# A mixer rewritten with its side work woven in by step, and shared kv, start and first mixers reordered, in a two-block float32 transformer kernel

## The reference

```python
for l in range(DEPTH):                                   # first block
    h = h + 0.5 * rmsnorm(swiglu(rmsnorm(h, g_pre_ffn1[l]), w_ffn1_gu[l], w_ffn1_down[l]), g_post_ffn1[l])
    h = h + rmsnorm(token_mixer(rmsnorm(h, g_pre_mix[l]), ...), g_post_mix[l])
    h = h + 0.5 * rmsnorm(swiglu(rmsnorm(h, g_pre_ffn2[l]), ...), g_post_ffn2[l])

for layer in range(DEPTH):                               # second block
    x = x + 0.5 * swiglu_2(rms_norm(x, ffn1_norm[layer]), ...)
    h, mem_n = rms_norm(x, mix_norm[layer]), rms_norm(mem, mem_norm[layer])
    x = x + (mlstm_mixer(h, mem_n, ...) if layer == 0 else dilated_mixer(h, mem_n, k_sh, v_sh, ...))
    x = x + 0.5 * swiglu_2(rms_norm(x, ffn2_norm[layer]), ...)
    if layer == 0:
        kv = rms_norm(x, kv_norm) @ w_kv                 # 1024 x 1536; k_sh normed per head, v_sh

def mlstm_mixer(h, mem_n, w_in, conv_w, gate_bias, h_gain, w_out, w_mem_kv, mq_gain, mk_gain):
    p = h @ w_in
    qk = silu(causal_conv(p[..., :2 * W], conv_w))       # W = 768, 4 taps
    v, o = p[..., 2 * W:3 * W], p[..., 3 * W:4 * W]
    gates = p[..., 4 * W:4 * W + 8] + gate_bias
    q_mem = p[..., 4 * W + 8:]
    cell = mlstm_chunkwise(heads(q), heads(k), heads(v), gates[..., :4], gates[..., 4:])
    h_a = sigmoid(o) * rms_norm(cell, h_gain)            # 4 heads of 192
    h_m = memory_cross_attention(q_mem, mem_n, w_mem_kv, mq_gain, mk_gain)
    return concatenate([h_a, h_m]) @ w_out
```

## Time and profile before

| | |
|---|---|
| three runs, us | 2742.65, 2736.28, 2741.81; median 2741.81 |
| profiled execution | 2741.48 us, span 2740.2 us |
| mean granted clock of TensorE in the span | 0.944 |
| bytes moved | 385.85 MB, mean 141 GB/s |
| ACT busy, DVE busy | 1236.9 us (45%), 1714.4 us (63%) |

### The profile page before, as it was taken

The page is one execution under the profiler, slowest core; times in us unless marked ns, Lnnn a source line. Parts: engine busy times, 40 slices in busy tenths (PEclk is TensorE's granted clock), DMA queues, the critical chain, the costliest instruction groups (busy, mean ns, idle before and its releaser), DMA issues.

```text
span 2740.2 us, 45911 instructions
## 1 busy us (share of the span) xinstructions
PE 2486.9 (91%) x18761; PEld 2345.7 (86%) x18761; DVE 1714.4 (63%) x3034; ACT 1236.9 (45%) x2101; POOL 33.5 (1%) x61
## 2 busy tenths in 40 slices
PE   7998898899999989989999986869998899868999
PEld 6997788799999977779999985758998899656999
DVE  5656667675575577667658645665764675354664
ACT  4444354454454435445446433334544554433543
POOL 2000000000000000000000000000000000000000
PEclk9998999899999999989999998878999999777999
DMA  6654433465465442356647643213755465511664
GB/s 182 176 177 118 109 86 109 117 183 177 138 186 177 136 121 78 97 142 178 189 143 200 186 136 81 75 37 91 200 185 154 125 188 188 160 44 54 185 186 138
DMA packets 589569, 385.85 MB, mean 141 GB/s; under 512 B 44555, under 2 KB 563951, under 8 KB 589232
## 3 DMA queue, kind: packets, MB, share of 16 engines
q1 hardware_dynamic: 585408, 374.00, 47.3%
q10 hardware_dynamic: 2176, 5.92, 0.6%
q0 software_dynamic: 1776, 2.98, 0.4%
HBM read 378.59 MB, written 4.19 MB: 140 GB/s over the span
## 4 chain that ended last, share of the span: by engine, by line
PE 71%; DVE 16%; ACT 6%; issue 5%; DMA 1%; SPq 0%; POOL 0%; DVEq 0%; ACTq 0%; POOLq 0%
PE bank L496 70%; DVE wlo L1674 4%; ACT whi L1130 3%; DVE a_qk L2200 1%; DVE ry L1692 1%; DVE ry L1690 1%; DMA wraw<-in_w_ffn_gu 1%; DVE stat_a L2090 1%; DVE ybuf L2088 1%; DVE smh L1950 0%; POOL g L438 0%; ACT rst L1151 0%; DVE smh L2114 0%; DVE rst L1694 0%; ACT a_qk L1512 0%
## 5 line engine op out<-in xcount | busy, mean ns | idle before, releaser
L1674 DVE TENSOR_TENSOR wlo<-wraw,whi 128x1024 fp32r<-128x1024 f32 (+3 forms) x723 | 868.7, 1207 | 433.5 <-ACT whi L1130 430.4
L1130 ACT ACTIVATE whi<-wraw 128x1024 fp32r<-128x1024 f32 (+3 forms) x723 | 748.1, 1042 | 613.2 <-DMA wraw<-in_w_ffn_gu 184.9
L496 PE MATMUL bank<-xhi,whi 128*128 128x256 f32 (+2 forms) x4024 | 617.0, 294 | 75.5 <-ACT xhi L1166 26.3
L496 PEld LDWEIGHTS bank<-xhi,whi 128*128 128x128 f32 (+1 forms) x4024 | 544.0, 193 | 101.2 <-ACT xhi L1166 30.0
L496 PE MATMUL bank<-xhi,wlo 128*128 128x256 f32 (+2 forms) x4024 | 598.5, 289 | 14.8 <-DVE wlo L1674 14.8
L496 PE MATMUL bank<-xlo,whi 128*128 128x256 f32 (+2 forms) x4024 | 582.7, 286 | 0.0
L496 PEld LDWEIGHTS bank<-xhi,wlo 128*128 128x128 f32 (+1 forms) x4024 | 542.3, 192 | 18.6 <-DVE wlo L1674 18.3
L496 PEld LDWEIGHTS bank<-xlo,whi 128*128 128x128 f32 (+1 forms) x4024 | 529.9, 189 | 0.2
L496 PE MATMUL bank<-act_hi,wlo 128*128 128x256 f32 (+1 forms) x1408 | 400.5, 284 | 0.0
L496 PE MATMUL bank<-act_lo,whi 128*128 128x256 f32 (+1 forms) x1408 | 400.5, 284 | 0.0
L496 PE MATMUL bank<-act_hi,whi 128*128 128x256 f32 (+1 forms) x1408 | 398.6, 283 | 0.0
(11 more groups left out here) (373 smaller groups left out, 1852.5 us busy)
## 6 DMA issues: line engine op xcount, KB each, us to landing
wraw<-in_w_ffn_gu SPq DMA_DIRECT2D x176, 512.0 KB, 3.9
wraw<-in_w_ffn_down SPq DMA_DIRECT2D x88, 512.0 KB, 3.2
wraw<-in_ffn_w_gate SPq DMA_DIRECT2D x88, 512.0 KB, 3.9
wraw<-in_ffn_w_up SPq DMA_DIRECT2D x88, 512.0 KB, 3.9
wraw<-in_ffn_w_down SPq DMA_DIRECT2D x88, 512.0 KB, 3.2
wraw<-in_w_in SPq DMA_DIRECT2D x80, 512.0 KB, 3.9
wraw<-in_a_w_in SPq DMA_DIRECT2D x24, 384.0 KB, 3.2
wraw<-in_w_out SPq DMA_DIRECT2D x16, 512.0 KB, 3.9
```

The source lines that it names most:

```text
L496: return E.matmul(out_, lhsT, rhs, start=first, stop=last, skip_group_check=True)
L1130: A.activation(flat(whi, u), flat(wraw, u), ACT.Copy).then_inc(S("hi"), 1)
L1674: V.tensor_tensor(flat(wlo, u), flat(wraw, u), flat(whi, u).bitcast(F32), ALU.subtract).then_inc(lo_ready[u % RING], 1)
```

## The change

Stage a is written anew. Its slabs have another order (`A_HEAD`, `A_ORDER`, `A_OUT`), by head; evictions go by `take`; turns, norms, gates, convs, silus, cells and memory attention are side chains, each bound to steps, on four `xb` buffers and buffers of their own for values and norms. Silus run once per head over two pairs of slabs. The o gate is a sigmoid on ACT over four slabs at a time. The cells keep their numerator in the bank, and the normalizer goes into the mean square, without a reciprocal. The memory attention is woven with the ao slabs. The first four aoc slabs are taken together, k by k. The split of the memory rows moves into f4 (j from 14 to 17).

Shared kv takes `KV_ORDER`, with six buffers for raw keys and squares, norms on two banks, turns on another. At the start the constants come in two parts and x in two, SP holds the third slab until they are in, only the first parameter block is turned (on its own semaphore `par1`), and x is turned k by k; the other two are turned in f0. In the mixers of the first block the alpha matmuls have banks 2 and 3, and the high and low parts stand in other places of the queues. DVE's `ahead` is one slab shorter. After stage b the low parts of f7's head come after the last `fill_low`.

```diff
+A_HEAD = [("ag", 0), ("aqk", 0), ("aqk", 1), ("aqk", 8)]
+A_ORDER = ([("aqk", 9), ("av", 0), ("aqk", 2), ("av", 1), ("aqk", 3), ("aqk", 10), ("mkv", 2), ("aqk", 11), ("aqk", 4), ("av", 2), ("aqk", 5),
+            ("aqk", 12), ("av", 3), ("aqk", 13), ("aqk", 6), ("av", 4), ("aqk", 7), ("aqk", 14), ("aq", 0), ("aqk", 15), ("mkv", 0), ("av", 5),
+            ("aq", 1), ("mkv", 1), ("mkv", 3)] + [("ao", i) for i in range(8)])
+A_OUT = [("aoc", 0), ("aoc", 1), ("aoc", 2), ("aoc", 3), ("aom", 0), ("aom", 1), ("aoc", 4), ("aoc", 5), ("aom", 2), ("aoc", 6), ("aoc", 7), ("aom", 3)]
+A_TAKEN = {key: i for i, key in enumerate(A_HEAD + A_ORDER)}
+A_CONV = [i for name, i in A_HEAD + A_ORDER if name == "aqk"]
...
+A_CONV_STEP = [2, 2, 3, 3] + [A_STEP["aqk", i] + 1 for i in A_CONV[4:]]
+A_CELL_STEP = (5, 12, 18, 24)
+A_MEM_STEP = 26
+A_NORM_BANK = (7, 7, 7, 2)
+KV_ORDER = [0, 1, 2, 3, 6, 4, 7, 5, 8, 9, 10, 11]
+KV_TURN = (3, 5, 7, 8, 9, 10)
 
...
                 Y.wait_ge(S("used"), u - RING + 1)
+            elif u == 2:
+                Y.wait_ge(S("in"), 64)
             for src, c0 in pieces:
...
-                        E.wait_ge(S("evac"), c.first + 1)
+                        E.wait_ge(S("evac"), c.first + 4)
                         for q in range(2):
-                            b = next_bank()
-                            mm(bank[b][:, 0:T1], wau[:, L, q * P:q * P + P], rst2[0:GATE_RANK, :], True, True).then_inc(S("wau"), 1)
+                            mm(bank[2 + q][:, 0:T1], wau[:, L, q * P:q * P + P], rst2[0:GATE_RANK, :], True, True).then_inc(S("wau"), 1)
...
+                E.wait_ge(S("a_cn"), 4)
+                E.wait_ge(S("a_rs"), 4)
+                E.wait_ge(S("hn_out"), hn0 + 4)
+                E.wait_ge(S("mem_e"), MEM_N)
+                E.wait_ge(S("evac"), c.proj)
+                us = [AT["aoc", 0, d] for d in range(4)]
+                for k in range(8):
+                    E.wait_ge(S("a_cellh"), k + 1)
+                    for d, u in enumerate(us):
+                        if k == 0:
+                            E.wait_ge(S("hi"), u + 1)
+                        mm(bank[d][:, 0:T], slab(whi, u)[:, k, :], cellp[0][R, k, :], k == 0, False)
+                    for d, u in enumerate(us):
+                        if k == 0:
+                            E.wait_ge(lo_ready[u % RING], u // RING + 1)
+                        mm(bank[d][:, 0:T], slab(wlo, u)[:, k, :], cellp[0][R, k, :], False, False)
+                    E.wait_ge(S("a_cellp"), k + 1)
+                    for d, u in enumerate(us):
+                        m = mm(bank[d][:, 0:T], slab(whi, u)[:, k, :], cellp[1][R, k, :], False, False)
+                        if k == 7:
+                            m.then_inc(S("used"), 1)
+                    yield
...
-        E.wait_ge(S("in"), 48)
-        turn_rows(xs, N_META, 2, 0)
-        turn_rows(xs, P, 0, 8)
-        turn_rows(xs, P, 1, 16)
-        E.wait_ge(S("par"), PAR_START)
-        for b, (src, rows, w) in enumerate(((g1, 108, P), (g2, 78, P), (g3, 72, MH))):
-            E.transpose(bank[b][0:w, 0:rows], src[0:rows, 0:w], ident[0:rows, 0:rows]).then_inc(S("gain_t"), 1)
+        E.wait_ge(S("in"), 64)
+        E.wait_ge(S("par1"), PAR_FIRST)
+        E.transpose(bank[0][0:P, 0:108], g1[0:108, :], ident[0:108, 0:108]).then_inc(S("gain_t"), 1)
+        turn_rows()
+        E.wait_ge(S("gains"), 1)
         for L in range(DEPTH):
...
                 hi_until(AT["gk", L, 1] + 1)
                 in_squares(f"m{L}", cols1, range(4, 8))
-                hi_until(AT["gk", L, 1] + 2)
+                hi_until(AT["gk", L, 1] + 3)
                 stat(cols1, 7)
                 c.proj += 5
-                ahead(("gk", L, 1))
                 yield
                 for i, (name, s) in enumerate([(name, s) for name in ("fq", "fk") for s in range(4)]):
-                    ahead((name, L, s))
+                    hi_until(AT["fq", L, 0] + min(2 * i + 4, i + 1 + LEAD))
                     c.proj += 1
...
-            for d in range(KD):
-                ahead(("wo", L, d))
             X = AT["g", 2 * L + 1, 0]
-            post(cols1 if L == 0 else cols2, lambda d: A.wait_ge(S("used"), AT["wo", L, d] + 1), X)
+            hi_until(X - 1)
+            post(cols1 if L == 0 else cols2, lambda d: A.wait_ge(S("used"), AT["wo", L, d] + 1),
+                 {4: X, 5: X + 1, 6: X + 2, 7: X + 3, 8: X + 4})
...
+                for n, (name, i) in enumerate(A_ORDER):
+                    hi_until(AT[name, 0, i] + min(n + 3, 1 + LEAD))
+                    if name == "aqk":
+                        tap(i)
+                    elif (name, i) in A_NORMS:
+                        A.wait_ge(S("evac"), taken((name, i)))
+                        A.activation(hsq[:, c.hn_sq % 2, :], hz[:, c.hn_sq % 2, :], ACT.Square).then_inc(S("hn_sq"), 1)
+                        c.hn_sq += 1
+                    if (name, i) == ("ao", 7):
+                        sigmoids(0)
...
+            def silus():
+                for h in range(ML_HEADS):
+                    while c.step < A_CONV_STEP[4 * h + 3]:
+                        yield
+                    A.wait_ge(S("a_conv"), 4 * h + 4)
                     table[0] = "silu"
-                    A.activation(a_qk[R, i, :], a_qk[R, i, :], ACT.Silu).then_inc(S("a_qk"), 1)
-                    yield
...
+                    A.activation(a_qk[R, 2 * h:2 * h + 2, :], a_qk[R, 2 * h:2 * h + 2, :], ACT.Silu)
+                    A.activation(a_qk[R, 8 + 2 * h:10 + 2 * h, :], a_qk[R, 8 + 2 * h:10 + 2 * h, :], ACT.Silu).then_inc(S("a_qk"), 1)
                     exp_ln()
...
-        A.dma_start(cst, IN["consts"]).then_inc(S("in"), 16)
+        A.dma_start(cst[:, 0:P], IN["consts"][:, 0:P]).then_inc(S("in"), 16)
         A.dma_start(xs[0:N_META, 2, :], IN["meta_tokens"]).then_inc(S("in"), 16)
-        A.dma_start(xs[:, 0:2, :], IN["x"][0].rearrange("(t p) d -> p t d", p=P)).then_inc(S("in"), 16)
+        for t in range(2):
+            A.dma_start(xs[:, t, :], IN["x"][0, t * P:t * P + P, :]).then_inc(S("in"), 16)
+        A.dma_start(cst[:, P:CONST_N], IN["consts"][:, P:CONST_N]).then_inc(S("cst"), 16)
         hi_until(2)
         A.wait_ge(S("eps"), 1)
         A.wait_ge(S("gains"), 1)
-        fill("f0", cols1, 0)
+        for k in range(KD):
+            if k == 1:
+                hi_until(3)
+            if k == 2:
+                hi_until(4)
...
-                    ahead((name, L, s))
+                    if i != 1:
...
                         for q in range(2):
                             V.wait_ge(S("wau"), 2 * L + q + 1)
-                            b = next_bank()
-                            V.tensor_scalar(cb[:, q, :], b[:, 0:T1], gain1[:, 96 + 2 * L + q:97 + 2 * L + q], None, ALU.add).then_inc(S("evac"), 1)
-                        V.wait_ge(S("evac"), c.proj)
+                            own(V.tensor_scalar(cb[:, q, :], bank[2 + q][:, 0:T1], gain1[:, 96 + 2 * L + q:97 + 2 * L + q], None, ALU.add))
+                        lo_until(AT["fq", L, 0] + 5)
+                        wait_own()
...
-            for d in range(KD):
-                ahead(("wo", L, d))
-            post("m", L, cols1 if L == 0 else cols2,
-                 f"f{2 * L + 1}", ffn_cols(2 * L + 1), AT["g", 2 * L + 1, 0])
+            X = AT["g", 2 * L + 1, 0]
+            lo_until(X - 1)
+            post("m", L, cols1 if L == 0 else cols2, f"f{2 * L + 1}", ffn_cols(2 * L + 1),
+                 {3: X, 4: X + 1, 5: X + 2, 6: X + 3, 7: X + HEAD})
...
+                for n, (name, i) in enumerate(A_ORDER):
+                    lo_until(AT[name, 0, i] + min(n + 3, LEAD))
+                    take(name, i)
+                    yield
...
+            def convs():
+                for n, i in enumerate(A_CONV):
+                    while c.step < A_CONV_STEP[n]:
+                        yield
...
-                        ins = V.scalar_tensor_tensor(y, xb[z][R, j:j + T], gain3[:, 8 + 16 * j + i:9 + 16 * j + i], y, ALU.mult, ALU.add)
+                        ins = V.scalar_tensor_tensor(y, xb[n % 4][R, j:j + T], gain3[:, 8 + 16 * j + i:9 + 16 * j + i], y, ALU.mult, ALU.add)
...
-                    V.reciprocal(o, o).then_inc(S("a_o"), 1)
...
+            def main():
+                begin(5)
+                add_squares(T, range(1, 4))
+                lo_until(AT["kv", 0, 0] + HEAD + 1)
+                add_squares(T, range(4, 7))
+                stat(cols2, 7)
+                for s in range(HEAD):
+                    take_k(s)
+                yield
+                for s in KV_ORDER[HEAD:]:
+                    ahead(("kv", 0, s))
+                    if s < 6:
+                        take_k(s)
+                    else:
+                        if s >= 8:
+                            V.wait_ge(S("tv_t"), c.tv - 1)
+                        b = took(("kv", 0, s))
+                        V.tensor_tensor(kzb[s % 2], b[:, 0:T], rs, ALU.mult).then_inc(S("evac"), 1)
+                        c.tv += 1
...
```

(4 more changed lines are left out.)

752 lines of the change are left out of this document (491 added, 261 removed).

## The result

The changed kernel takes 2572.39 us in the median of 4 runs (2569.13 to 2574.36), the kernel before 2742.23 in 4 runs (2736.28 to 2743.09): a ratio of 0.9384, with a 95% interval from 0.9367 to 0.9400. That is 170 us less; I had forecast 125 less and a range that ends at 2592. The sign was right, and each of the stretches that I had named moved the way I said; the size was not right.

What follows compares the result with a forecast made beforehand. The prediction took PE (TensorE), busy 91%, as the bound, with its pauses and half clock to be won. Its terms, -82 - 15 - 10 - 8 - 12 + 2 = -125 us, gave 2617 from about 2741.8, range 2592 to 2655.

Steps and rivals of the forecast that it cites:

- The start: Kernel start: x lands earlier and only the first gain is turned; 8 us less, between 3 and 11.
- The gate wait: First block's mixers, PE's wait for the decay's cumulative sum: 5 us less each, keeping a stall of 2.
- The end of the mixers: First block's mixers: squares start while PE still computes, so the next feed-forward starts 7.5 us earlier each.
- Moving DVE's lookahead from 5 slabs to 4 everywhere: All stages: costed at 0 where PE waits for nothing; in the dilated mixer it could be 4 either way.
- Stage a: Second block's first mixer: floor 175 us plus 32.8 of losses, about 208, so 82 us less.
- coupling of 15 us: Woven steps of stage a: loss taken because DVE's work is longer than PE's in some steps; 15 us.
- Shared kv: Shared kv stage: two norm banks and own buffers remove waits; 54 us against 66, 12 less (8 to 16).
- The last feed-forward: Last feed-forward: low part of its last head slab now follows the last fill; 2 us more (0 to 4).
- A: Rival, woven steps of stage a: DVE and PE do not overlap; stage a 240 us, time 2649; chance 0.20.
- B: Rival, table switches in stage a: ACT is late after each burst, 11 us, time 2628; chance 0.09.
- C: Rival, stage a: PE's clock falls to half between slabs; stage a 368 us, time 2776, slower; chance 0.02.
- D: Rival, parts outside stage a: they do nothing, the 43 us are lost but for kv's 12; 2648; chance 0.05.

Runs made afterwards that it cites:

- a_fqold: Changed kernel with the first block's mixers' gate part (alpha banks, places of high and low parts) as before: 2573.94 us, mixers 239.68 and 238.56.
- a_post1: Changed kernel with the old end of the first block's mixers, high parts of 8 slabs ahead of the squares: mixers 244.03 and 242.21 us.
- b_lead: Kernel before with only DVE's lookahead one slab shorter everywhere: 2697.96 us, against 2739.82 for the kernel before beside it.
- v1_f7: Changed kernel with the dilated mixer's output loop making DVE's low parts one slab further ahead, before the last fill: 2568.64 us, ratio 0.9375 to the kernel before.
- a_dist0: Changed kernel with DVE's low parts one slab further ahead in stage a alone: stage a 221.5 us.
- v3_acthi: v1_f7 with ACT's high parts one slab further ahead where they go by the lookahead: 2571.40 us.

## Why the prediction was right or wrong

**The start (-8, measured -3.3)** was mis-sized. PE turned the first gain at 12.17 and not at 11, and its first steady matmul came at 23.8, not 20.3: the chain copy, high part, low part by k takes about 0.9 us for each of the last k, which I had put beside each other. Until 28.5 four matmuls then took 1.11 us, against 0.67 behind it, though the profile gives the granted clock as 1.00 in both.

**The gate wait (-5 each)** went as forecast as far as the kernel before is compared with the change (5.3 us between the mean square and the first matmuls of the decay chain in the first mixer), but by a_fqold only 3 of it are the gate part's own. The stall of 2 that I kept is two waits of 4.3 us together, on DVE's `qa`.

**The end of the mixers (-7.5 each)** was right: 7.4 and 6.9 by a_post1, though the handover of 0.7 in its sum is not there.

**The step that failed** is "Moving DVE's lookahead from 5 slabs to 4 everywhere is 0 where PE waits for nothing". I treated the lookahead as a margin for PE. It is also what binds two other queues: at the old bounds DVE's low part and ACT's high part of one slab stood at the same step. It is worth 13 us in each mixer (b_lead; 14 in reverse), where I had put it at nothing, and 25 in the old stage a. These 26 to 28 us are most of the 35 missed in the mixers. The earlier trace rows had it in the line that I used for the price of a low part: 17.9 us idle before it, released by ACT's high parts, beside 21.1 us of work. I read that line's mean and not its idle column, since DVE is not the bound; but PE was waiting for DVE in the earlier trace rows.

**Stage a (-82, measured -85.1, or -84 to -92 with the scatter)** was right in its sum and partly by luck. The coupling of 15 us is 0. In its place the side work is dearer: the fp32 forms sum to 54 us where I had taken 42, with the clock at 1.00 through the middle of the stage (1610 to 1710). The single losses that I kept came close: 3.3 after the mean square (3.5 forecast), 2.3 before the output (2.2), 0.7 at the head (1.6).

**Shared kv (-12, measured -19.3)** was mis-sized: I left 4 us where DVE makes a low part behind four evictions, 3.2 at the head and 3 of half clock. PE's waits in the stage sum to 2.4 us, and its clock was 1.00.

**The last feed-forward (+2, measured +3.6)** had the right cause, by v1_f7; I had left out the slower clock after the pause.

**The rivals.** A (no overlap in the woven steps) did not happen, though a_dist0 shows how near it was: one slab of lookahead more and 14 to 22 us of it come back. B had the wrong place: the silus lie on the chain to the cells, not in front of the high parts. In the change they cost 2.9 us once. C did not happen; the clock in stage a is 0.93. D was wrong in the other direction.

**Two figures of the prediction don't follow from its own terms.** Rival C turns the sign when about 140 of the 175 us run at half, not 148 (290.5 + 43 - 18 - 175 = 140.5). And with all parts at their bounds the forecast's range is 2589 to over 2650, not 2592 to 2640. The measured 2572 lies below either.

## What to carry to other kernels

Where two engines make a slab's two halves one after the other, try a lookahead for the second that is one slab shorter than the first's; here, with equal ones, the second stood in its queue in front of work that others waited for, and its longer lookahead cost where it seemed to buy margin. In the kernel before, moving the first engine further ahead did more (2684.8 us) than holding the second back (2698.0); a second slab of distance gave nothing (v3_acthi). Read the idle column of the engine that releases the bound engine, not only that of the bound one. And look at how many small waits remain beside the large ones: here 12 kinds, none above 3.1 us, were 18 us in a mixer, and one edit took 9 of them away.
